# Up projection of a two-layer transformer block as seven products of quarters instead of eight

## What is computed

```python
xn2 = rmsnorm(x, norm2_g)
x = x + jnp.square(jax.nn.relu(xn2 @ w_up)) @ w_down
# x: 512 x 1024, w_up: 1024 x 4096, w_down: 4096 x 1024
```

## Time and profile before

| | |
|---|---|
| median of 3 runs | 1969.43 us |
| fastest and slowest of them | 1969.37 and 1969.91 us |
| span of the profiled execution | 1967.4 us |
| own time of the profiled execution | not given apart from its span; the median is 2.0 us above the span |
| TensorE busy | 1959.2 us (100%), 9686 matmuls |
| VectorE, ScalarE, GpSimd busy | 1024.1, 764.9, 83.8 us |
| mean granted TensorE clock | 0.999 of 2.4 GHz |
| DMA | 183 MB, 93 GB/s on average |

### The profile page before, as it was taken

How to read it: one execution, slowest core, us unless ns; L and a number is a source line. 1 busy time by engine, 2 the same in 40 slices (tenths; PEclk the granted TensorE clock), 3 DMA queues, 4 the chain that set the end, 5 groups by cost and what they waited for, 6 DMA issues and landing times.

```text
span 1967.4 us, 23153 instructions
## 1 busy us (share of the span) xinstructions
PE 1959.2 (100%) x9686; PEld 1614.8 (82%) x9686; DVE 1024.1 (52%) x1394; ACT 764.9 (39%) x1226; POOL 83.8 (4%) x132
## 2 busy tenths in 40 slices
PE   9999999999999999999999999999999999999998
PEld 8888888888888888888888888888888888887776
DVE  5553466435453436643334355545554447596675
ACT  5556563332323333442134232222222321447864
POOL 0000000000000000000000000000000000005541
PEclk9999999999999999999999999999999999999999
DMA  6222222223122242233233323232323334521011
GB/s 214 84 68 85 65 86 75 86 91 106 65 91 86 87 148 86 86 107 108 86 105 89 106 86 107 86 107 89 105 86 107 86 124 114 152 81 44 23 55 65
DMA packets 184295, 183.36 MB, mean 93 GB/s; under 512 B 5120, under 2 KB 159232, under 8 KB 184192
## 3 DMA queue, kind: packets, MB, share of 16 engines
q1 hardware_dynamic: 179840, 172.15, 28.2%
q10 hardware_dynamic: 4352, 9.75, 1.6%
HBM read 175.59 MB, written 4.19 MB: 91 GB/s over the span
## 4 chain that ended last, share of the span: by engine, by line
PE 98%; ACT 1%; DVE 0%; DMA 0%; issue 0%; POOL 0%; DVEq 0%; ACTq 0%
PE bank L1403 85%; PE bank L1630 2%; PE bank L1611 2%; PE bank L1644 2%; PE bank L1501 1%; PE bank L1490 1%; PE bank L1529 1%; PE bank L1413 1%; ACT raw L1663 0%; PE bank L1464 0%; PE bank L1433 0%; PE bank L1509 0%; PE bank L1577 0%; PE bank L1446 0%; PE bank L1620 0%; PE bank L1431 0%
## 5 line engine op out<-in xcount | busy, mean ns | idle before, releaser
L1403 PE MATMUL bank<-xh,wh 128*128 128x512 f32 x1352 | 534.1, 395 | 0.0
L1403 PE MATMUL bank<-xh,wl 128*128 128x512 f32 x1352 | 527.6, 390 | 0.0
L1403 PE MATMUL bank<-xl,wh 128*128 128x512 f32 x1352 | 527.0, 390 | 0.0
L1680 ACT CAST wh<-raw 128x2048 fp32r<-128x2048 f32 (+2 forms) x151 | 279.5, 1854 | 408.8 <-PE bank L1403 405.1
L2234 DVE TENSOR_TENSOR wl<-raw,wh 128x2048 fp32r<-128x2048 f32 (+2 forms) x151 | 335.0, 2221 | 169.5 <-ACT wh L1680 169.3
L1403 PEld LDWEIGHTS bank<-xh,wl 128*128 128x128 f32 x1352 | 253.4, 187 | 53.8
L1403 PEld LDWEIGHTS bank<-xh,wh 128*128 128x128 f32 x1352 | 253.7, 188 | 50.3
L1403 PEld LDWEIGHTS bank<-xl,wh 128*128 128x128 f32 x1352 | 253.8, 188 | 50.0
L1403 PE MATMUL bank<-wh,xh 128*128 128x512 f32 x320 | 129.4, 404 | 0.0
L1403 PE MATMUL bank<-wh,xl 128*128 128x512 f32 x320 | 125.1, 391 | 0.0
L1403 PE MATMUL bank<-wl,xh 128*128 128x512 f32 x320 | 125.1, 391 | 0.0
(11 more groups left out here) (325 smaller groups left out, 2925.8 us busy)
## 6 DMA issues: line engine op xcount, KB each, us to landing
raw<-in_w_in SPq DMA_DIRECT2D x49, 1024.0 KB, 5.0
raw<-in_a_w_in SPq DMA_DIRECT2D x32, 1024.0 KB, 5.5
raw<-in_w_up SPq DMA_DIRECT2D x16, 1024.0 KB, 5.3
raw<-in_w_down SPq DMA_DIRECT2D x16, 1024.0 KB, 5.8
raw<-in_w_proj_b SPq DMA_DIRECT2D x8, 1024.0 KB, 5.1
raw<-in_a_w_out SPq DMA_DIRECT2D x8, 1024.0 KB, 5.7
raw<-in_w_out SPq DMA_DIRECT2D x4, 1024.0 KB, 5.2
raw<-in_w_kv SPq DMA_DIRECT2D x4, 1024.0 KB, 4.9
```

Of the source, the lines that this page charges most:

```text
L1403: m = e.matmul(o, p, q, start=k == 0 and n == 0, stop=k == K - 1 and n == 2)
L1680: m = e.copy(hi, r)
```

## The change

The 1024x4096 matrix `w_up` is cut in 8 groups q = 4f + g of 512 features. A group's weights (1024x512) are cut in four quarters of 512x256: two halves of the rows (k) by two of the columns (n). The activations are cut in four as well: two halves of k by two halves of the tokens, T. Four output pieces (256 features by 256 tokens, names "nT": 11, 12, 21, 22) then come from seven products (n = 1 to 7) of quarters or of sums and differences of quarters.

- **TensorE** (`seven`): each product is 2 tiles by 4 blocks by 3 = 24 matmuls with 256 moving columns, summed into half banks. 8 groups of 7 products replace 32 tiles of 24 matmuls with 512 columns.
- **Sums of weights**: four of the seven products take a sum of quarters. These are made in DRAM (`sums`) by 64 DMAs of 512 KB on GpSimd's queue, half of them with `accum_op=ALU.add`, each waiting for the one four before it. They begin after tile ("q", 0, 3).
- **Weights in SBUF**: `raw`, `wh` and `wl` are used as 6 and 4 halves of 128x1024 during the up projection; each product has a half of its own (`part`). ScalarE casts each; the low parts of products 2, 6 and 3 are subtracted by GpSimd, behind its 64 DMAs in its queue, those of the other four by VectorE.
- **Sums of activations**: made by VectorE in `wo`: one operation of 256 columns for tiles 0 to 3, three (`x_less`, `x_least`, sum) for tiles 4 to 7; ScalarE casts 256 or 768 more columns, VectorE subtracts as many (`xeh`, `xel`).
- **Results**: running sums in PSUM are copied by ScalarE at three points of a group (`shot`), combined by VectorE (`piece_sum`), then relu, `rs`, square, cast and subtraction as before, now by piece (`piece`, `piece_low`).
- `ROOT[1]` is 2: the sum of squares stands behind the third product. Semaphore names of other stages are merged; nothing else there changes.

```diff
+SEVENS = [(0, 1), (1, 1), (2, 1), (0, 2), (1, 2), (0, 7), (1, 7), (0, 6), (1, 6), (0, 5), (1, 5), (0, 3), (0, 4),
+          (1, 3), (1, 4), (3, 1), (2, 2), (3, 2), (2, 7), (3, 7), (2, 6), (3, 6), (2, 5), (3, 5), (2, 3), (2, 4),
+          (3, 3), (3, 4)]
+LOW_ON_POOL = (2, 6, 3)
...
-        for c in range(8):
-            chunk(("up", f, c), "w_up", 0, 8, f * 2048 + c * 256, 256)
-            for j in range(2):
-                col(("up", f, c, j), ("up", f, c), j * 128, 8, ("x", 1), "out_d")
+        for g, n in SEVENS:
+            if n in SUM_OF:
+                chunk(("seven", f, g, n), SUM_OF[n], f * 4 + g, 4, 0, 256, "sum")
+            else:
+                chunk(("seven", f, g, n), "w_up", 512 * (n != 1), 4, f * 2048 + g * 512 + 256 * (n == 4), 256, "quarter")
...
-    split = [t for t in o if k == 7 and t[0] in ("w", "w_piece")]
+    split = [t for t in o if k == 7 and t[0] in ("w", "w_piece", "part")]
...
+def sevens(f):
+    out, low = [], []
+    for i, (g, n) in enumerate(SEVENS):
+        out.append(("seven", f, g, n))
+        if f == 0 and i == ROOT[1]:
+            out += [("sum_squares", 1), ("root", 1)]
+        out += low
+        if n in (2, 6, 5):
+            out.append(("shot", f, g, 1 if n == 2 else n))
+        if n in PIECE_OF:
+            out.append(("piece_sum", f, g, PIECE_OF[n]))
+        out += after_chunk(("seven", f, g, n))
+        if n in PIECE_OF:
+            out.append(("piece", f, g, PIECE_OF[n]))
+        low = [("piece_low", f, g, PIECE_OF[n])] if n in PIECE_OF else []
+    return out + low
...
+        def seven(f, g, n):
+            into = INTO[n]
+            if n in (1, 2, 7):
+                take("st" + into, ("st", f, g, into), ("st_out", f, g, into))
+            else:
+                w.wait_ge(*(told("st_out", f, g, "22") if n == 4 else told("shot", f, g, {6: 1, 5: 6, 3: 5}[n])))
+            bank = bank_of("st" + into, ("st", f, g, into))
+            w.wait_ge(*told("pool_lo" if n in LOW_ON_POOL else "lo", ("seven", f, g, n)))
...
+                    for x, (p, q) in enumerate(((hi, h), (hi, l), (lo, h))):
+                        m = e.matmul(bank[:, t * 256:(t + 1) * 256], p[:, c], q,
...
+            stt(v[:, 0:256], xT[:, k - 4, 256:512], v_("norm2_g", k - 4), t[:, 256:512], ALU.mult, ALU.subtract).then_inc(
+                *tell("x_sum", k, "x_less"))
...
+            stt(v[:, 256:512], xT[:, k - 4, 0:256], minus_g[:, k - 4:k - 3], v[:, 0:256], ALU.mult, ALU.add).then_inc(
+                *tell("x_sum", k, "x_least"))
...
+            e.tensor_tensor(v[:, 512:768], t[:, 0:256], v[:, 256:512], ALU.add).then_inc(*tell("x_sum", k))
...
+        w.wait_ge(*told("tile", ("q", 0, 3)))
+        for each in SUM_STEPS:
+            sum_weights(*each)
+        def part(f, g, n):
+            if n in LOW_ON_POOL:
+                name = "seven", f, g, n
+                w.wait_ge(*told("hi", name))
+                hi, lo = split_half(name)
+                e.tensor_tensor(lo, raw_half(name), hi, ALU.subtract).then_inc(*tell("pool_lo", name))
```

More of the change, by code:

```diff
@@ L222, in after_chunk @@
 def after_chunk(name):
[L224 to L228, removed]
+    out = []
+    for new in AFTER.get(name, []):
+        if new[0] == "seven":
+            out.append(("part", *new[1:]))
+        elif new in PIECES:
+            out += [("w_piece", new, x) for x in range(4)]
+        elif name not in LATE and new not in PIECED:
+            out.append(("w", NTH[new]))
+    return out
 LATE = (("vsw", 0), ("vsw", 1))
-PIECES = (("wo", 1), ("up", 0, 2))
+PIECES = (("wo", 1),)
 PIECED = (("q", 0, 1), ("bo", 0, 0), ("bo", 0, 1), ("bo", 1, 0), ("bo", 1, 1), *PIECES)
@@ L423, in some @@
             for x in t:
-                if x[0] == "mm" and ends_chunk(*x[1:]) and AFTER[ends_chunk(*x[1:])] in PIECED:
-                    pieces.extend(("w_piece", AFTER[ends_chunk(*x[1:])], y) for y in range(4))
+                if x[0] == "mm" and ends_chunk(*x[1:]):
+                    pieces.extend(("w_piece", new, y) for new in AFTER.get(ends_chunk(*x[1:]), ()) if new in PIECED for y in range(4))
         del fill[:n]
@@ L1383, in mm @@
                     w.wait_ge(*told("xl", 0, *x_part(b, k)))
+            elif ready == "hl":
+                for event in h_pieces(xs[1], k):
+                    w.wait_ge(*told(*event))
             else:
@@ L1685, in w_piece, with shot, piece @@
             w.wait_ge(*told(f"raw{SLOT[n]}", n))
-            if name in BEFORE:
-                w.wait_ge(*told(*chunk_read(BEFORE[name])))
+            for old in BEFORE.get(name, ()):
+                w.wait_ge(*told(*chunk_read(old)))
             c = slice(x * 512, x * 512 + 512)
             e.copy(wh[WSLOT[name]][:, c], raw[SLOT[n]][:, c]).then_inc(*tell("hi", name, x))
+        def part(f, g, n):
+            name = "seven", f, g, n
+            w.wait_ge(*told(f"half{SLOT[PLACE[name]]}", name))
+            for old in BEFORE[name]:
+                w.wait_ge(*told(*chunk_read(old)))
+            e.copy(split_half(name)[0], raw_half(name)).then_inc(*tell("hi", name))
+        def shot(f, g, n):
+            piece = SHOT[n]
+            w.wait_ge(*told("tile", ("seven", f, g, n)))
+            if piece_before(f, g, piece):
+                w.wait_ge(*told("hl", *piece_before(f, g, piece)))
+            elif piece == "11":
+                w.wait_ge(*told("xl", 1, 6 + g, "sums"))
+            else:
+                w.wait_ge(*(told("sum_square", 1, 7) if piece == "21" else told("ssq", 1)))
+            e.copy(shot_place(g, piece)[:, :], bank_of("st12", ("st", f, g, "12"))[:, :]).then_inc(*tell("shot", f, g, n))
+        def piece(f, g, c):
+            t = shot_place(g, c)
+            w.wait_ge(*(told("st_out", f, g, c) if c == "12" else told("st_out", f, g, c, "relu")))
+            act(t[:, :], t[:, :], ACT.Square).then_inc(*tell("up_sq", f, g, c))
+            if f:
+                w.wait_ge(*told("tile", ("down", 0, 7, 0)))
+            else:
+                after("mix")
+            w.wait_ge(*told("up_sq", f, g, c))
+            e.copy(h_part(hh, g, c), two(t[:, :])).then_inc(*tell("hh", f, g, c))
         def w_part(k):
@@ L2583, in b_ @@
             w.wait_ge(*told("out_d", key))
[L2584 removed]
+            e.tensor_tensor(t[:, :], t[:, :], rs[:, :], ALU.mult).then_inc(*tell("conv", "b", f))
         def z(c, j):
```

374 lines of the change are left out of this document (253 added, 121 removed).

## The result

The changed kernel takes **1984.98 us** (median of 4 runs, 1980.31 to 1986.94), the kernel before beside it 1969.40: a ratio of 1.0075, 95% interval 1.0063 to 1.0087, so **slower** by 0.75% where 0.4% faster was forecast. The profiled execution took 1983.26 us with a span of 1981.3, 13.9 us longer than the span before.

A forecast was written before the change was run, and what follows sets the result against it. The prediction took the up projection as bound by TensorE's matmuls alone. 1967.4 - 15.4 + 5.4 + 1.5 + 1 = 1959.9 us span, with 2.0 us for the median 1962 us; range 1953 to 1972.

The forecast's parts named there:

- Term 4: Body of the up projection and change to down: small waits for results and weights, +1 us, bounds 0 and 3.
- up to 5.1 us each costs nothing: Body of the up projection: GpSimd's subtractions, taken as up to 2.5 us each, stay hidden up to 5.1 us.
- waits all through the body: Up projection: if GpSimd's and VectorE's operations can't overlap, 1980 us, chance 0.11 slower; just below, 1969, 0.12 no change.
- P: GpSimd's time for one subtraction; without overlap a group needs 12.0 + 3P us on GpSimd and VectorE, against 19.8.
- Nothing else there changes ... 0: Other stages: issues, merged semaphore names and the removed wait on `x_raw` lie in no critical queue, cost 0.
- Term 1: Up projection on TensorE: 1344 matmuls at 0.118 us replace 174.0 us by 158.6, -15.4 us.
- Term 2: Entry to the up projection: TensorE waits once for VectorE's late subtraction of the third product's weights, 5.4 us, bounds 0 and 8.
- Term 3: Just after the entry's wait: a while at 1.2 GHz slows matmuls, +1.5 us, bounds 0 and 3.
- The sum DMAs at 0: From near 30 to 825 us: the 64 DMAs of weight sums, 5 to 15 us each, stay hidden behind matmuls, cost 0.

The follow-up runs named there:

- dve_lows: The changed kernel with all seven low parts subtracted by VectorE and none by GpSimd: 1973.59 us, ratio 1.0020 to the kernel before.
- bank_phase: The changed kernel with the main PSUM bank ring stepped on by 16 behind each half of the up projection: 1975.58 us, ratio 1.0033 to the kernel before.
- banks_dve: The changed kernel with the ring stepped on by 16 behind each half and all low parts on VectorE: 1967.13 us, ratio 0.9987 to the kernel before.
- no_x_sums: The changed kernel with products 7, 6 and 4 on plain activation quarters, sums for tiles 4 to 7 left out (output differs): 1976.92 us, one run.
- all_three: banks_dve with two products' weight splits moved ahead of wo's last-tile work and the sum of squares behind the fourth product: 1961.55 us, ratio 0.9959.
- before_sums: The kernel before with the 64 weight-sum DMAs added on GpSimd's queue, their result unused: 1969.48 us, ratio 1.0000.
- entry_ahead: The changed kernel with two products' weight splits moved ahead of wo's last-tile work and the sum of squares behind the fourth product: 1981.51 us, ratio 1.0060.

## Why the prediction was wrong

- **Which step failed.** Term 4, in its sentence on GpSimd: "up to 5.1 us each costs nothing". The price was nearly right: 2.5 us taken, 2.62 measured in the mean (2.40 undisturbed; 22 of the 24 between 2.39 and 2.82, the two that met a subtraction of VectorE's from its start 3.36). But the sum held GpSimd's time against TensorE's deadline alone, and VectorE's 12.0 us a group as though they lay beside it. In place of +1 us for the whole term the changed trace has 12.1: waits of 8.5 us behind the entry (14.8 - 6.3), and slow starts of 3.6 (5.7 - 2.1). GpSimd's part is 11.4 us in the medians (`dve_lows`; 8.5 with the banks put back, `bank_phase` less `banks_dve`).
- **The rival that held the mechanism** was "waits all through the body". Its threshold (P = 2.6 us) was met by a mean of 2.62. The rule of the Trainium skill stood beside it. That its 1980 us is only 5 below the outcome is luck: that time was worked out for P = 3.4, and at 2.62 its own sum gives an excess of under 0.1 us a group, for which it named 1969. The 5.9 us in the tail aren't in it at all. Its chance, 0.11 for slower and 0.12 for no change, was too low for a mechanism that no row excluded, with a price at the threshold. Its working was also too smooth: it summed the pair's work over a group. The loss comes before the pair is full, at one product in each half, through a relu held for 2.56 us, ScalarE's queue behind it and the cast that GpSimd itself needs.
- **"Nothing else there changes ... 0".** The cost of moving a stage off a shared ring of banks was not seen at all: the wait in `compress` and the clock behind it cost 5.9 us 500 us later, and `bank_phase`, which also shortens the second exit, gives back 9.4 in the medians. The diff shows no line there. This alone would have used up most of the forecast gain.
- **Term 1** was right in kind and 2.7 us too good: 0.120 us for 0.118, so -12.7 for -15.4, inside the bounds. The four loads of the earlier trace rows, 0.1175 us apart, were no better guide than the rule that both lengths now give: 512 columns at 2.4 GHz are 0.2133 us and take 0.2266, 256 are 0.1067 and take 0.120, each 13.3 ns more. The forecast had 0.2266 in its hands and could have tried this with it.
- **Term 2** was right: 5.4 us forecast, 6.3 measured as a distance between starts. The chain came out as worked: adds of tiles 4 to 7 at 801.4, 806.5, 814.0 and 819.0 (forecast 801.3, 806.2, 813.5, 818.4), the subtraction done at 827.1 (826.2). `no_x_sums` and `all_three` show the cause.
- **Term 3** (+1.5) was the right effect at one place, 2.1 us: 21 slow starts, most of them 0.093 us too far apart, where at most 0.107 was taken. It was not applied to shorter waits, where it came too: 1.5 us each behind waits of 2.3 and 2.2 us, and a part of the 5.9 in the tail. So a wait cost up to 1.7 times its own length.
- **The account** of the profiled span, 1981.3 for 1959.9: term 1 +2.7, term 2 +0.9, term 3 +0.6, term 4 +11.1, the tail +5.9; 21.2 of 21.4 us.
- **The sum DMAs at 0** were right (`before_sums`); in the changed kernel they landed in 10.2 us in the median (48 that read `w_up`) and 7.7 (16 that read sums), where 5 to 15 were taken.

Not tried: a version in which GpSimd works with other inputs, so that the exclusion doesn't bite, and a free choice of banks in `compress` in place of the stepped ring.

## What to carry to other kernels

Before work is moved from VectorE to GpSimd, count it on both: here GpSimd's subtractions held back the VectorE operations with two SBUF inputs that started beside them, and it was the queues behind a held one that reached TensorE. When a stage stops or starts to take from a shared ring of buffers, put the ring back to its old phase behind it, and read the trace up to the end of the kernel. A product scheme that saves an eighth of the columns but issues 1344 matmuls in place of 768 pays the fixed cost of each; here it left 12.7 us of the 21.8 (174.0 / 8) that the columns alone promise.

## What was not expected of the hardware

- A matmul of these operands costs its columns at 2.4 GHz plus 13.3 ns, with 256 and 512 columns alike (0.120 and 0.2266 us). At 1.2 GHz the surplus isn't there: 0.213 and 0.427 us are 256 and 512 columns at that clock.
- The lower clock (1.2 GHz) followed waits of only 2.2 us (mean granted clock 0.67 in 1083 to 1087), and began 1.3 us behind the wait's end there. It did not follow each wait of that length: behind the first wait for GpSimd at 884.6 the clock stayed at 1.00, behind its like in the second half came 17 slow starts. In `entry_ahead` both were followed by slow starts.
- The Trainium skill ("SBUF — State Buffer", SBUF: two separate sides) says that the one of the two operations that starts first gets the shared ports for the whole instruction and the other fully blocks. The rows agree in who loses, and add a price: VectorE's held relu ended 0.55 us after GpSimd's subtraction did, where alone it takes 0.69 in all; GpSimd's, met by a relu already under way, lost 0.35 us, and up to 0.96 beside a subtraction of VectorE's.
